# Two weight chunks in one matrix instruction for most tiles of queries, z and output; VectorE takes part in the last splits

## The chip, the cores and the metric

One core of a Trainium2 chip runs the whole kernel. The metric is device time in microseconds, the median of several executions. Every duration below is of one profiled execution.

## The reference, cut to what matters

One layer, 1024 tokens of width 1024, all float32. A normalised h (1024 x 1024) is multiplied by one wide weight matrix w_in whose columns are split into eleven parts; two branches follow and are merged:

```python
proj = h @ w_in[layer]
(u_a, z_a, q, k, v, z_b, q_idx, k_idx, w_idx, g_a, g_b) = jnp.split(proj, split_points, axis=-1)
y_a = multiscale_pool(u_a, ...) * silu(z_a)
q = rope(rmsnorm(q)); k = rope(rmsnorm(k)); q_idx, k_idx = rope(q_idx), rope(k_idx)
attn = dsa_sparse_attention(q, k, v, q_idx, k_idx, w_idx)   # scores with relu, top 256 keys, softmax
y_b = attn * silu(z_b)
merged = sigmoid(g_a) * (y_a @ w_branch_a) + sigmoid(g_b) * (y_b @ w_branch_b)
x = x + gate * (merged @ w_out)
```

q and z_b have 512 columns each, w_out is 1024 x 1024.

## The kernel before, in words

**Numbers in two parts.** Every float32 operand of a large product is split into a high part (rounded by a copy into the matrix format) and a low part (the rest). A product is three matrix instructions, high x high, high x low, low x high (lines 680 to 682, function `product`). For weights, ScalarE makes the high part (line 617, `split_piece_hi`) and GpSimd the low part (line 622, `split_piece_lo`); VectorE does it for the first four pieces alone (`split_piece_v`).

**Chunks, pieces, slots.** Weights come in chunks of 256 columns (`CW`), numbered in the order of use; a chunk of 1024 rows is two pieces of 128 x 4 x 256, loaded by SyncE into one of three raw buffers (`load_piece`), which is free again once the low part is made. The parts of a chunk stand in slot (ci - 1) % 2 of `w_hi` and `w_lo`. So chunk ci + 2 can be split only when the last product with chunk ci is done (`chunk_done`, waited for in `split_chunk_hi`). The two chunks of q, the two of z_b, and w_out's chunks 0 and 1, and 2 and 3, are neighbours and fill slots 0 and 1.

**Tiles of rows.** For q, z_b and the output, 128 tokens are the stationary operand and 256 weight columns the moving one: 8 steps of k, three instructions each, into half of a PSUM bank. The banks `pp[0]` and `pp[1]` alternate; a list `pp_uses` fixes the order of their uses, and `pp_claim` waits until the last user of the bank was evicted. The other products (`channels`) have weights as stationary and 512 tokens as moving operand.

**Order of the stages on TensorE.** (1) k, v and the index parts. (2) Scoring: six blocks b = 2 to 7 of eight heads each. A head is one product of index queries with (b + 1) x 128 keys into `ps`; ScalarE applies relu (line 1209), VectorE adds it into the score (lines 1850, 1853). After each head TensorE does two steps of a q tile (`q_step`, `Q_STEPS` = 2): 16 steps, two narrow tiles, a block. At head 5 it transposes the index queries of the next block (line 809), which GpSimd must have split (`qi_split_lo`, line 1458), in its queue behind the finishing of a q tile (`finish_query`), which follows VectorE's normalisation of that tile, whose last step is `query_gain` (line 1840) at head 7. (3) z_b: all eight tiles of chunk 0, then all eight of chunk 1; ScalarE applies silu (line 1176) and stores them to memory; after four tiles it takes square roots for the last four query tiles, which VectorE and GpSimd then finish before VectorE begins the bisection for the 256th score (line 1877). GpSimd's queue here is: low parts of z chunk 0, the causal select of the last scores (line 1489, waits for VectorE's last score), low parts of z chunk 1, the last query tiles, low parts of ua 0 and gb 0. (4) 20 chunks of h products (ua, gb, za, ga), the tie masks in between (`mask_products`; VectorE writes `eq`, line 1912, TensorE transposes it, line 885). (5) Attention. (6) Branch b: 16 units of 12 wide instructions; VectorE merges each (lines 1984 and 1986), ScalarE makes the high part of the merged unit (`mT_hi`, line 1393), GpSimd its low part (`mT_lo`, line 1627). m_raw has four buffers, freed by the low part. (7) Output: four chunks one after another, eight tiles each; TensorE first waits for 14 of the 16 merged units. VectorE multiplies by the gate (line 2028, this frees the bank), adds the row of x (line 2031), ScalarE issues the store. The splits of the next chunks are ScalarE's and GpSimd's.

Of the kernel before, what the change touches and what calls it, by code (L numbers as in the profile page):

```python
# [23 lines left out]
P = 128  # L24
# [15 lines left out]
CW = 256  # L40
# [26 lines left out]
def hybrid_layer(nc, x, c, positions, w_ada, b_ada, norm_gain, w_in, w_pool_group, pool_scale,  # L67
# [106 lines left out]
    for i in range(4):  # L174
        pp_uses += [("wo", i, t) for t in range(NT)]
# [17 lines left out]
    def chunk_done(ci):  # L193

        name = [k for k, v in name_of.items() if v == ci][0]
        kind, i = name if isinstance(name, tuple) else (name, 0)
        return max(pp_sig[n] for n, use in enumerate(pp_uses)
                   if use[:2] == (kind, i) or (kind == "za" and use[:2] == ("mix", i)))
# [48 lines left out]
    with ExitStack() as ctx:  # L247
# [78 lines left out]
        def tenants_a(s):  # L326
# [12 lines left out]
            with ExitStack() as k:  # L339
                zb_out = alloc(k, "zb_out", [P, 4, CW])  # L340
# [4 lines left out]
        def tenants_c(s):  # L345
# [10 lines left out]
            with ExitStack() as k:  # L356
                x_row, o_row = alloc(k, "x_row", [P, 4, CW]), alloc(k, "o_row", [P, 4, CW])
# [77 lines left out]
        m_raw_done, mT_hi_done, mT_lo_done = sem("m_raw_done"), sem("mT_hi_done"), sem("mT_lo_done")  # L435
# [30 lines left out]
        def _(sp):  # L466
# [70 lines left out]
            def load_x_row(n):  # L537
                i, t = n // NT, n % NT
                if n >= 4:
                    sp.wait_ge(o_row_done, n - 3)  # L540
                sp.dma_start(x_row[:, n % 4, :], x[t * P:(t + 1) * P, i * CW:(i + 1) * CW]).then_inc(x_row_in[n % 4], 16)
# [10 lines left out]
            for i in range(4):  # L552
                sp.wait_ge(zb_spilled[i], 16 * 4)
# [96 lines left out]
        Q_STEPS = 2  # L650
        assert Q_STEPS * NSEL * H == (2 * NT - Q_FIRST) * KD
# [7 lines left out]
        def _(pe):  # L659
# [24 lines left out]
            def rows_step(o, t, ci, k, width):  # L684

                s, tok = slot(ci), slice(t * P, (t + 1) * P)
                if ci == name_of["kv"]:
# [3 lines left out]
                               w_hi[:, s, k, 0:width], w_lo[:, s, k, 0:width], k == 0, k == KD - 1)  # L691

# [128 lines left out]
            def q_step(n):  # L821
                (i, t), k = Q_ORDER[n // KD], n % KD
                ci = name_of[("q", i)]
# [3 lines left out]
                last = rows_step(o, t, ci, k, CW)  # L827
# [201 lines left out]
            pe.wait_ge(mT_lo_done, 14)  # L1029
            for i in range(4):  # L1030
                ci = name_of[("wo", i)]
                pe.wait_ge(w_lo_done, pieces_through[ci])
                for t in range(NT):
                    if i == 0 and t == NT // 2:
                        pe.wait_ge(mT_hi_done, 16)
                        pe.wait_ge(mT_lo_done, 16)
                    o = pp_claim(("wo", i, t))
                    tok = slice(t * P, (t + 1) * P)
                    for k in range(KD):
                        last = product(o[:, 0:CW], mT_hi[:, k, tok], mT_lo[:, k, tok], w_hi[:, slot(ci), k, :],  # L1040
                                       w_lo[:, slot(ci), k, :], k == 0, k == KD - 1)
                    last.then_inc(pp_full, 1)
# [3 lines left out]
        def _(act):  # L1046
# [124 lines left out]
            def zb_tile(i, t):  # L1171
                s = (i * NT + t) % 4
                if i * NT + t >= 4:
                    act.wait_ge(zb_spilled[s], 16 * ((i * NT + t) // 4))
# [26 lines left out]
            for b in range(FREE_BLOCKS, NT):  # L1201
                for h in range(H):
# [14 lines left out]
                    step += Q_STEPS  # L1217
# [16 lines left out]
            for s in range(4):  # L1234
                act.wait_ge(zb_spilled[s], 16 * 4)
# [173 lines left out]
        def _(pool):  # L1409
# [98 lines left out]
            for s in range(4):  # L1508
                pool.wait_ge(zb_spilled[s], 16 * 4)
# [119 lines left out]
            for i in range(4):  # L1629
                split_chunk_lo(pool, name_of[("wo", i)] + 2)  # L1630
# [3 lines left out]
        def _(dve):  # L1634
# [182 lines left out]
            def query_squares(t):  # L1817
                dve.wait_ge(pp_free_a, pp_at[("q", 1, t)] + 1)
# [233 lines left out]
```

## Time and profile before

| | us |
|---|---|
| median of 3 runs | 843.44 (843.12 to 843.59) |
| the profiled execution | 841.9 |
| its span, first to last instruction | 839.7 |
| TensorE busy | 803.0 (96%) |
| VectorE busy | 569.2 (68%) |
| GpSimd busy | 380.6 (45%) |
| ScalarE busy | 351.2 (42%) |

The profiled time is the span and 2.2 us around it. In the rows, PE is TensorE's matmuls, PEld its weight loads, DVE VectorE, ACT ScalarE, POOL GpSimd, SP SyncE. Matmul records overlap, since the engine is pipelined: the distance from start to start is the pace. "[1.08 <-issue]" at a row's end is the idle time before it and what ended it.

### The profile page before, as it was taken

The numbers are of one execution on the slowest core, as the hardware profiler recorded it, in microseconds if no ns is written. First come the engines' busy times: TensorE is split into PE (matmuls) and PEld (weight loads), VectorE is DVE, ScalarE is ACT, GpSimd is POOL, SyncE is SP. The second block draws the span as 40 slices with busy tenths as digits, with TensorE's granted clock in tenths as the row PEclk, the third lists the DMA queues.
The fourth block names the chain that finished last, engine by engine and source line by source line (L and its number), as shares of the span: only waits on it lengthen the run. The fifth ranks groups of instructions, "written<-read, shape, count | busy, mean of one in ns | idle before, by whom it ended". The sixth has DMA issues, their size and how long they took to land.

```text
span 839.7 us, 13949 instructions
## 1 busy us (share of the span) xinstructions
PE 803.0 (96%) x4978; PEld 707.9 (84%) x4978; DVE 569.2 (68%) x1193; ACT 351.2 (42%) x647; POOL 380.6 (45%) x333
## 2 busy tenths in 40 slices
PE   3899999999999999999999999989999999999998
PEld 3699998889998888887878877778788887889998
DVE  5845538978888888898898636446557885654332
ACT  6473346665222222223242223676777883420000
POOL 1024544335624467861652212754887812982200
PEclk9899999999999999999999999999999999999999
DMA  9930110004332220331122323632433114744332
GB/s 350 378 90 14 51 51 14 27 13 126 124 102 64 90 79 32 98 99 42 51 88 88 100 98 117 218 122 89 141 110 95 46 37 140 247 138 135 120 93 73
DMA packets 62685, 87.95 MB, mean 105 GB/s; under 512 B 5881, under 2 KB 44317, under 8 KB 61726
## 3 DMA queue, kind: packets, MB, share of 16 engines
q1 hardware_dynamic: 48606, 64.04, 24.5%
q10 hardware_dynamic: 12096, 16.78, 5.6%
q0 software_dynamic: 1920, 6.29, 2.0%
q8 instruction: 40, 0.66, 0.3%
q14 instruction: 23, 0.19, 0.1%
HBM read 66.12 MB, written 20.97 MB: 104 GB/s over the span
## 4 chain that ended last, share of the span: by engine, by line
PE 86%; ACT 4%; DVE 3%; DMA 3%; issue 2%; SPq 1%; POOL 0%; DVEq 0%; ACTq 0%
PE pp L680 23%; PE pp L682 22%; PE pp L681 22%; PE pp L1007 3%; PE ps L818 3%; PE ps L817 3%; PE pt L973 3%; DMA ada_w<-in_w_ada 2%; ACT a_out L1311 1%; SPq L490 1%; DVE prob L1998 1%; DVE pT L1940 1%; PE ps L749 1%; PE pt L919 1%; ACT w_hi L617 1%
## 5 line engine op out<-in xcount | busy, mean ns | idle before, releaser
L622 POOL TENSOR_TENSOR w_lo<-w_raw,w_hi 128x1024 fp32r<-128x1024 f32 x50 | 123.6, 2490 | 216.8 <-ACT w_hi L617 165.1
L1877 DVE TENSOR_SCALAR_CACHE_REDUCE junk<-score,cand 128x384 uint8<-128x384 f32 (+1 forms) x186 | 168.6, 944 | 19.3 <-issue 13.3
L680 PE MATMUL pp<-hT_hi,w_hi 128*128 128x512 f32 x384 | 150.2, 391 | 0.0
L682 PE MATMUL pp<-hT_hi,w_lo 128*128 128x512 f32 x384 | 149.5, 389 | 0.0
L681 PE MATMUL pp<-hT_lo,w_hi 128*128 128x512 f32 x384 | 149.4, 389 | 0.0
L680 PE MATMUL pp<-w_hi,hT_hi 128*128 128x256 f32 x352 | 101.2, 287 | 0.5 <-ACT zb_out L1176 0.5
L682 PE MATMUL pp<-w_hi,hT_lo 128*128 128x256 f32 x352 | 99.4, 282 | 0.0
L681 PE MATMUL pp<-w_lo,hT_hi 128*128 128x256 f32 x352 | 99.4, 282 | 0.0
L1940 DVE TENSOR_TENSOR pT<-pt,pT 128x512 fp32r<-128x512 f32 (+3 forms) x96 | 50.5, 554 | 53.2 <-ACT pT L1361 50.4
L680 PEld LDWEIGHTS pp<-hT_hi,w_hi 128*128 128x128 f32 x384 | 72.1, 188 | 16.0 <-issue 0.8
L682 PEld LDWEIGHTS pp<-hT_hi,w_lo 128*128 128x128 f32 x384 | 72.1, 188 | 15.2
L681 PEld LDWEIGHTS pp<-hT_lo,w_hi 128*128 128x128 f32 x384 | 72.1, 188 | 14.7
L680 PE MATMUL pp<-w_hi,mT_hi 128*128 128x256 f32 x256 | 72.5, 283 | 0.6 <-ACT mT_hi L1393 0.6
L617 ACT ACTIVATE w_hi<-w_raw 128x1024 fp32r<-128x1024 f32 x52 | 52.6, 1052 | 47.6 <-DVE o_row L2031 43.4
L681 PE MATMUL pp<-w_lo,mT_hi 128*128 128x256 f32 x256 | 72.4, 283 | 0.0
L682 PE MATMUL pp<-w_hi,mT_lo 128*128 128x256 f32 x256 | 72.4, 283 | 0.0
L1247 ACT ACTIVATE stage<-pp 128x512 f32<-128x512 f32 x32 | 19.1, 598 | 126.7 <-PE pp L682 126.7
L680 PEld LDWEIGHTS pp<-w_hi,hT_hi 128*128 128x128 f32 x352 | 67.1, 191 | 1.6 <-ACT zb_out L1176 0.7
L681 PEld LDWEIGHTS pp<-w_lo,hT_hi 128*128 128x128 f32 x352 | 67.2, 191 | 0.7
L682 PEld LDWEIGHTS pp<-w_hi,hT_lo 128*128 128x128 f32 x352 | 67.1, 191 | 0.0
L680 PE MATMUL pp<-yT_hi,w_hi 128*128 128x512 f32 x128 | 52.5, 410 | 1.1 <-ACT a_out L1311 1.1
L1853 DVE SCALAR_TENSOR_TENSOR score<-rel,w_idx,score 128x384 f32<-128x384 f32 (+5 forms) x42 | 46.8, 1114 | 10.0 <-ACT rel L1209 6.6
(275 smaller groups left out, 1817.2 us busy)
## 6 DMA issues: line engine op xcount, KB each, us to landing
w_raw<-in_w_in SPq DMA_DIRECT2D x36, 512.0 KB, 3.8
ada_w<-in_w_ada SPq DMA_DIRECT2D x7, 1024.0 KB, 11.6
sgb_spill<-stage ACTq DMA_DIRECT2D x16, 256.0 KB, 2.0
sga_spill<-stage ACTq DMA_DIRECT2D x16, 256.0 KB, 2.0
stage<-sga_spill SPq DMA_DIRECT2D x16, 256.0 KB, 3.2
ma_spill<-stage POOLq DMA_DIRECT2D x16, 256.0 KB, 2.4
gate_w<-in_w_ada SPq DMA_DIRECT2D x16, 256.0 KB, 2.7
w_raw<-in_w_out SPq DMA_DIRECT2D x8, 512.0 KB, 4.5
```

The lines of the kernel that those rows point to most:

```text
L617: nc.scalar.activation(hi, raw, ACT.Copy).then_inc(w_hi_done, 1)
L622: nc.gpsimd.tensor_tensor(lo, raw, hi.bitcast(F32), ALU.subtract).then_inc(w_lo_done, 1)
L680: nc.tensor.matmul(o, a_hi, b_hi, start=first, stop=False)
L681: nc.tensor.matmul(o, a_hi, b_lo, start=False, stop=False)
L682: return nc.tensor.matmul(o, a_lo, b_hi, start=False, stop=last)
L817: nc.tensor.matmul(o[:, a:z], q, kt_[:, 0, a:z], start=True, stop=False)
L818: last = nc.tensor.matmul(o[:, a:z], q, kt_[:, 1, a:z], start=False, stop=True)
L973: last = nc.tensor.transpose(o[:, (t % 4) * P:(t % 4 + 1) * P], prob[j % 4][:, t * P:(t + 1) * P], ident[:])
L1007: last = nc.tensor.matmul(pp[0][:, 0:2 * P], v2[:, t, :], pT[:, u % 2, t, s, :, :].rearrange("p h q -> p (h q)"), start=(t == 0 and s == 0 ...
L1853: ins = v.scalar_tensor_tensor(s, rel[:, n % 2, 0:keys(b)], w, s, ALU.mult, ALU.add)
L1877: v.tensor_scalar(junk[:, n % 2, 0:keys(b)], score[:, score_at(b):score_at(b + 1)], least, None, ALU.is_ge, ALU.add, accum_out=cnt[:, n:n ...
L1940: v.tensor_tensor(pT[:, j // 2 % 2, t0:t1, 1, j % 2, :], pt[n % 2][:, 0:(t1 - t0) * P].rearrange("p (t q) -> p t q", q=P), pT[:, j // 2 % ...
```

## The change

For tiles 2 to 6 of q, 2 to 7 of z_b and 2 to 7 of the output (for w_out's chunks 0 and 1, then 2 and 3), one instruction takes both slots as moving operand: 512 columns, two pieces of 256 in `w_hi[:, :, k, :]`, into a whole bank (`pair_step`). The others stay narrow and stand around the pairs: of z_b (0,0), (0,1) ahead and (1,0), (1,1) behind; of the output the same for each pair of chunks. During scoring a head of blocks 2 to 6 has one wide step instead of two narrow ones; block 7 keeps two narrow ones. Evictions, row buffers (`zb_out`, `x_row`, `o_row`), loads and stores of pairs have 512 columns. ScalarE splits ua 0 after the last z pair. The low parts of merged units with odd number, and of w_out's chunks 1, 2 and 3, go from GpSimd to VectorE; VectorE makes those of chunk 2 just ahead of evicting the last pair of chunks 0 and 1, those of chunk 3 ahead of evicting tile (1, 1). GpSimd's queue around z_b is as it was.

```diff
-    Q_ORDER = [(0, 0), (0, 1), (1, 0), (1, 1)] + [(i, t) for t in range(2, NT) for i in range(2)]
+    BOTH = (0, 1)
+    Q_ORDER = [(0, 0), (0, 1), (1, 0), (1, 1)] + [(BOTH, t) for t in range(2, NT - 1)] + [(0, NT - 1), (1, NT - 1)]
     Q_FIRST = 4
     pp_uses += [("q", i, t) for i, t in Q_ORDER]
-    for i in range(2):
-        pp_uses += [("zb", i, t) for t in range(NT)]
+    ZB_ORDER = [(0, 0), (0, 1)] + [(BOTH, t) for t in range(2, NT)] + [(1, 0), (1, 1)]
+    pp_uses += [("zb", i, t) for i, t in ZB_ORDER]
+    ZB_SLOTS = [16 * len(ZB_ORDER[s::4]) for s in range(4)]
+    WO_ORDER = []
+    for i in (0, 2):
+        WO_ORDER += [(i, 0), (i, 1)] + [((i, i + 1), t) for t in range(2, NT)] + [(i + 1, 0), (i + 1, 1)]
+
+    def first_of(i):
+        return i[0] if isinstance(i, tuple) else i
+
+    def width_of(i):
+        return 2 * CW if isinstance(i, tuple) else CW
...
-        m_raw_done, mT_hi_done, mT_lo_done = sem("m_raw_done"), sem("mT_hi_done"), sem("mT_lo_done")
+        m_raw_done, mT_hi_done = sem("m_raw_done"), sem("mT_hi_done")
+        mT_lo_v, mT_lo_p = sem("mT_lo_v"), sem("mT_lo_p")
...
-            for n in range(4 * NT - 4):
-                if n == 4:
+            for n in range(len(WO_ORDER) - 4):
+                if n == 2:
                     load_piece(nxt)
                     load_piece(nxt + 1)
-                if n == NT + 4:
+                if n == 7:
                     for m in range(nxt + 2, len(pieces)):
                         load_piece(m)
                 load_x_row(n + 4)
...
-        Q_STEPS = 2
-        assert Q_STEPS * NSEL * H == (2 * NT - Q_FIRST) * KD
+        Q_STEPS = {b: 1 if b < NT - 1 else 2 for b in range(FREE_BLOCKS, NT)}
+        assert sum(Q_STEPS.values()) * H == (len(Q_ORDER) - Q_FIRST) * KD
...
+            def pair_step(o, act_hi, act_lo, t, k):
+
+                tok = slice(t * P, (t + 1) * P)
+                return product(o[:], act_hi[:, k, tok], act_lo[:, k, tok], w_hi[:, :, k, :], w_lo[:, :, k, :],
+                               k == 0, k == KD - 1)
...
-                last = rows_step(o, t, ci, k, CW)
+                last = pair_step(o, hT_hi, hT_lo, t, k) if i == BOTH else rows_step(o, t, ci, k, CW)
...
-                    for _ in range(Q_STEPS):
+                    for _ in range(Q_STEPS[b]):
...
-            for i in range(2):
-                for t in range(NT):
-                    rows_tile("zb", i, t, first=t == 0)
+            for i, t in ZB_ORDER:
+                if i != BOTH:
+                    rows_tile("zb", i, t, first=(i, t) == (0, 0))
+                    continue
+                pe.wait_ge(w_lo_done, pieces_through[name_of[("zb", 1)]])
+                o = pp_claim(("zb", i, t))
+                for k in range(KD):
+                    last = pair_step(o, hT_hi, hT_lo, t, k)
+                last.then_inc(pp_full, 1)
...
-            pe.wait_ge(mT_lo_done, 14)
-            for i in range(4):
-                ci = name_of[("wo", i)]
-                pe.wait_ge(w_lo_done, pieces_through[ci])
-                for t in range(NT):
-                    if i == 0 and t == NT // 2:
-                        pe.wait_ge(mT_hi_done, 16)
-                        pe.wait_ge(mT_lo_done, 16)
-                    o = pp_claim(("wo", i, t))
-                    tok = slice(t * P, (t + 1) * P)
-                    for k in range(KD):
+            pe.wait_ge(mT_lo_v, 7)
+            pe.wait_ge(mT_lo_p, 7)
+            for i, t in WO_ORDER:
+                pair = isinstance(i, tuple)
+                ci = name_of[("wo", i[-1] if pair else i)]
+                if t == (2 if pair else 0):
+                    pe.wait_ge(w_lo_done, pieces_through[ci])
+                if t == NT // 2:
+                    pe.wait_ge(mT_hi_done, 16)
+                    pe.wait_ge(mT_lo_v, 8)
+                    pe.wait_ge(mT_lo_p, 8)
+                o = pp_claim(("wo", i, t))
+                tok = slice(t * P, (t + 1) * P)
+                for k in range(KD):
+                    if pair:
+                        last = pair_step(o, mT_hi, mT_lo, t, k)
+                    else:
                         last = product(o[:, 0:CW], mT_hi[:, k, tok], mT_lo[:, k, tok], w_hi[:, slot(ci), k, :],
                                        w_lo[:, slot(ci), k, :], k == 0, k == KD - 1)
-                    last.then_inc(pp_full, 1)
+                last.then_inc(pp_full, 1)
...
-            for i in range(2):
-                for t in range(NT):
-                    zb_tile(i, t)
-                    if (i, t) == (0, 3):
-                        for late in NORM_LATE:
-                            query_root(late)
-                split_chunk_hi(act, name_of[("zb", i)] + 2)
+            for n in range(len(ZB_ORDER)):
+                zb_tile(n)
+                if n == 3:
+                    for late in NORM_LATE:
+                        query_root(late)
+                if n == len(ZB_ORDER) - 3:
+                    split_chunk_hi(act, name_of[("zb", 0)] + 2)
+            split_chunk_hi(act, name_of[("zb", 1)] + 2)
...
-            for n in range(4 * NT):
-                i, t = n // NT, n % NT
+            for n, (i, t) in enumerate(WO_ORDER):
+                if i == BOTH and t == NT - 1:
+                    split_chunk_hi(act, name_of[("wo", 2)])
+                if (i, t) == (1, 1):
+                    split_chunk_hi(act, name_of[("wo", 3)])
                 act.wait_ge(o_row_done, n + 1)
-                act.dma_start(out[t * P:(t + 1) * P, i * CW:(i + 1) * CW], o_row[:, n % 4, :]).then_inc(stored[n % 4], 16)
-                if t == NT - 1:
-                    split_chunk_hi(act, name_of[("wo", i)] + 2)
+                c0, w = first_of(i) * CW, width_of(i)
+                act.dma_start(out[t * P:(t + 1) * P, c0:c0 + w], o_row[:, n % 4, 0:w]).then_inc(stored[n % 4], 16)
...
-                if n in WB_LAST:
+                if n in WB_LAST and n < 15:
                     split_chunk_lo(pool, name_of[("wb", WB_LAST[n])] + 2)
-                pool.wait_ge(mT_hi_done, n + 1)
-                gp.tensor_tensor(mT_lo[:, 2 * i + m, tok], m_raw[:, n % 4, :], mT_hi[:, 2 * i + m, tok].bitcast(F32),
-                                 ALU.subtract).then_inc(mT_lo_done, 1)
-            for i in range(4):
-                split_chunk_lo(pool, name_of[("wo", i)] + 2)
...
-                    dve.wait_ge(mT_lo_done, n - 3)
+                    dve.wait_ge(*((mT_lo_v, (n - 3) // 2) if n % 2 else (mT_lo_p, (n - 2) // 2)))
...
+            def merge_low(n):
+                i, m, f = UNITS_B[n]
+                tok = slice(f * HALF, (f + 1) * HALF)
+                dve.wait_ge(mT_hi_done, n + 1)
+                v.tensor_tensor(mT_lo[:, 2 * i + m, tok], m_raw[:, n % 4, :], mT_hi[:, 2 * i + m, tok].bitcast(F32),
+                                ALU.subtract).then_inc(mT_lo_v, 1)
+
+            def split_chunk_v(ci):
+                for n, (cj, _) in enumerate(pieces):
+                    if cj == ci:
+                        dve.wait_ge(w_lo_done, n)
+                        split_piece_v(n)
...
+                if n % 2 == 0:
+                    merge_low(n - 1)
+            merge_low(15)
+            split_chunk_v(name_of[("wo", 1)])
+
+            for n, (i, t) in enumerate(WO_ORDER):
+                if i == BOTH and t == NT - 1:
+                    split_chunk_v(name_of[("wo", 2)])
+                if (i, t) == (1, 1):
+                    split_chunk_v(name_of[("wo", 3)])
+                u = pp_at[("wo", i, t)]
+                c0, w = first_of(i) * CW, width_of(i)
+                if (i, t) in ((0, 0), (2, 0)):
+                    dve.wait_ge(pt_free_a, pt_done[pt_at[("gate", i // 2)]][0])
...
-                v.tensor_tensor(o_row[:, n % 4, :], pp[pp_bank[u]][:, 0:CW], gate[:, i * CW:(i + 1) * CW],
+                v.tensor_tensor(o_row[:, n % 4, 0:w], pp[pp_bank[u]][:, 0:w], gate[:, c0:c0 + w],
                                 ALU.mult).then_inc(pp_free_v, 1)
                 dve.drain()
-                v.tensor_tensor(o_row[:, n % 4, :], o_row[:, n % 4, :], x_row[:, n % 4, :], ALU.add).then_inc(o_row_done, 1)
+                v.tensor_tensor(o_row[:, n % 4, 0:w], o_row[:, n % 4, 0:w], x_row[:, n % 4, 0:w], ALU.add).then_inc(o_row_done, 1)
```

## Rows read from the trace of the kernel before

**Rows 1.** Page, part 4: the chain that ended last, by engine.

```profile
PE 86%; ACT 4%; DVE 3%; DMA 3%; issue 2%; SPq 1%; POOL 0%; DVEq 0%; ACTq 0%
```

**Rows 2.** Windows: stretch, length, busy (instructions) of each engine, clock, DMA share, GB/s.

```profile
142.00:155.00 13.00, 12.38 (x93) 11.56 (x92) 11.88 (x20) 7.89 (x14) 5.31 (x7) 1.00 0.06 22
```

**Rows 3.** Timeline of TensorE before and in the output: start, length, line, operands.

```profile
737.84 0.39 PE L680 MATMUL pp<-yT_hi,w_hi 128*128 128x512 f32 x1
...
742.60 0.39 PE L680 MATMUL pp<-yT_hi,w_hi 128*128 128x512 f32 x1
...
744.46 0.28 PE L680 MATMUL pp<-w_hi,mT_hi 128*128 128x256 f32 x1
...
747.69 0.28 PE L680 MATMUL pp<-w_hi,mT_hi 128*128 128x256 f32 x1
```

**Rows 4.** Timeline, three engines, 168 to 176 us: end of scoring block 5.

```profile
168.69 0.68 DVE L1840 TENSOR_TENSOR q_all<-q_all,gains 128x512 f32<-128x512 f32 x1
...
173.87 1.27 POOL L1458 TENSOR_TENSOR qi_stk<-qi,qi_stk 128x512 fp32r<-128x512 f32 x1
...
175.24 0.84 PE L809 MATMUL pt<-ident_r,qi_stk 128*128 128x128 f32 x8 [1.08 <-issue]
```

**Rows 5.** Timeline, VectorE and GpSimd, 195 to 248 us.

```profile
195.05 2.67 DVE L1853 SCALAR_TENSOR_TENSOR score<-rel,w_idx,score 128x1024 f32<-128x1024 f32 x2
...
197.93 0.78 POOL L1489 TENSOR_SCALAR_AFFINE_SELECT score<-score 128x128 f32<-128x128 f32 x1 [4.07 <-DVEq L1858]
...
198.69 5.26 POOL L622 TENSOR_TENSOR w_lo<-w_raw,w_hi 128x1024 fp32r<-128x1024 f32 x2
...
242.62 4.77 POOL L622 TENSOR_TENSOR w_lo<-w_raw,w_hi 128x1024 fp32r<-128x1024 f32 x2 [13.73 <-ACT w_hi L617]
```

**Rows 6.** Timeline of TensorE at its third z tile.

```profile
199.98 0.38 PE L680 MATMUL pp<-w_hi,hT_hi 128*128 128x256 f32 x1 [0.45 <-ACT zb_out L1176]
```

**Rows 7.** Instructions on the tie masks eq: duration min/median/max, first and last start.

```profile
L885 PE MATMUL pt<-ident_b,eq x33: 219/219/230, 487.3 to 521.3; 128*128 128x128 bf16 x33
...
L1912 DVE TENSOR_SCALAR eq<-score,thr x6: 414/582/750, 474.6 to 519.8; 128x384 bf16<-128x384 f32 x1, 128x512 bf16<-128x512 f32 x1, 128x640 bf16<-128x640 f32 x1, 128x768 bf16<-128x768 f32 x1
```

**Rows 8.** Timeline, ScalarE and GpSimd, around the last tiles of z 0.

```profile
217.60 0.38 ACT L1176 ACTIVATE zb_out<-pp 128x256 f32<-128x256 f32 x1 [2.50 <-PE pp L682]
...
218.45 2.01 ACT L617 ACTIVATE w_hi<-w_raw 128x1024 fp32r<-128x1024 f32 x2 [0.46 <-ACT zb_out L1176]
...
241.49 2.01 ACT L617 ACTIVATE w_hi<-w_raw 128x1024 fp32r<-128x1024 f32 x2 [0.46 <-ACT zb_out L1176]
...
256.93 0.60 ACT L1259 ACTIVATE ua<-pp 128x512 f32<-128x512 f32 x1 [4.84 <-PE pp L682]
...
224.13 4.76 POOL L622 TENSOR_TENSOR w_lo<-w_raw,w_hi 128x1024 fp32r<-128x1024 f32 x2
```

**Rows 9.** Timeline, all four engines, last merge and first output tile.

```profile
739.25 5.94 POOL L1627 TENSOR_TENSOR mT_lo<-m_raw,mT_hi 128x512 fp32r<-128x512 f32 x4
...
743.48 2.01 ACT L617 ACTIVATE w_hi<-w_raw 128x1024 fp32r<-128x1024 f32 x2
...
743.48 0.69 DVE L1984 TENSOR_TENSOR m_raw<-pp,e_in 128x512 f32<-128x512 f32 x1 [0.69 <-PE pp L682]
...
744.03 0.36 PE L680 MATMUL pp<-w_hi,mT_hi 128*128 128x256 f32 x1 [0.59 <-ACT mT_hi L1393]
...
744.27 1.47 DVE L1986 TENSOR_TENSOR m_raw<-m_raw,e_in 128x512 f32<-128x512 f32 x1
...
745.77 0.63 ACT L1393 ACTIVATE mT_hi<-m_raw 128x512 fp32r<-128x512 f32 x1 [0.27 <-DVE m_raw L1986]
```

**Rows 10.** Instructions that write w_lo, VectorE's: duration min/median/max in ns.

```profile
L1708 DVE TENSOR_TENSOR w_lo<-w_raw,w_hi x2: 1218/1222/1225, 47.8 to 50.0; 128x1024 fp32r<-128x1024 f32 x2
```

**Rows 11.** Windows (columns of rows 2): the stretch of the lower clock.

```profile
40.00:46.00 6.00, 5.68 (x28) 5.71 (x29) 5.27 (x11) 5.76 (x11) 0.00 (x0) 0.54 0.26 75
```

**Rows 12.** Waits of TensorE: us in total, times, longest us.

```profile
PE ps L988 <- ACT oT L1338: 5.5, 6, 1.4
```

More of the change, by code:

```diff
@@ L173, in hybrid_layer @@
     pp_uses += [("wb", i, (m, f)) for i, m, f in UNITS_B]
-    for i in range(4):
-        pp_uses += [("wo", i, t) for t in range(NT)]
+    pp_uses += [("wo", i, t) for i, t in WO_ORDER]
     pp_bank += [(n + 1) % 2 for n in range(len(pp_uses) - len(pp_bank))]
@@ L197, in chunk_done @@
         return max(pp_sig[n] for n, use in enumerate(pp_uses)
-                   if use[:2] == (kind, i) or (kind == "za" and use[:2] == ("mix", i)))
+                   if use[:2] == (kind, i) or (kind == "za" and use[:2] == ("mix", i))
+                   or (use[0] == kind and isinstance(use[1], tuple) and i in use[1]))
     pt_uses = [("cols", "v"), ("gains", "v")]
@@ L339, in tenants_a @@
             with ExitStack() as k:
-                zb_out = alloc(k, "zb_out", [P, 4, CW])
+                zb_out = alloc(k, "zb_out", [P, 4, 2 * CW])
             alloc(s, "zone_k", [P, 8 * 256])
@@ L356, in tenants_c @@
             with ExitStack() as k:
-                x_row, o_row = alloc(k, "x_row", [P, 4, CW]), alloc(k, "o_row", [P, 4, CW])
+                x_row, o_row = alloc(k, "x_row", [P, 4, 2 * CW]), alloc(k, "o_row", [P, 4, 2 * CW])
             alloc(s, "zone_c", [P, 16 * 256])
@@ L552, in _ @@
             for i in range(4):
-                sp.wait_ge(zb_spilled[i], 16 * 4)
+                sp.wait_ge(zb_spilled[i], ZB_SLOTS[i])
             load_q(0)
@@ L822, in q_step @@
                 (i, t), k = Q_ORDER[n // KD], n % KD
-                ci = name_of[("q", i)]
+                ci = name_of[("q", first_of(i))]
                 if t == 0 and k % 4 == 0:
@@ L1169, in qi_copies, with zb_tile @@
                                          ACT.Copy).then_inc(pt_free_a, 1)
[L1171 to L1174, printed above, removed]
+            def zb_tile(n):
+                (i, t), s = ZB_ORDER[n], n % 4
+                c0, w = first_of(i) * CW, width_of(i)
+                if n >= 4:
+                    act.wait_ge(zb_spilled[s], 16 * (n // 4))
                 o = pp_take(("zb", i, t))
-                nc.scalar.activation(zb_out[:, s, :], o[:, 0:CW], ACT.Silu).then_inc(pp_free_a, 1)
+                nc.scalar.activation(zb_out[:, s, 0:w], o[:, 0:w], ACT.Silu).then_inc(pp_free_a, 1)
                 act.wait_ge(pp_free_a, pp_at[("zb", i, t)] + 1)
-                act.dma_start(zb_dram[t * P:(t + 1) * P, i * CW:(i + 1) * CW], zb_out[:, s, :]).then_inc(zb_spilled[s], 16)
+                act.dma_start(zb_dram[t * P:(t + 1) * P, c0:c0 + w], zb_out[:, s, 0:w]).then_inc(zb_spilled[s], 16)
             for i, t in LATE:
@@ L1216, in _ @@
                         qi_copies(b + 1)
-                    step += Q_STEPS
+                    step += Q_STEPS[b]
                     if step % KD == 0:
@@ L1234, in _ @@
             for s in range(4):
-                act.wait_ge(zb_spilled[s], 16 * 4)
+                act.wait_ge(zb_spilled[s], ZB_SLOTS[s])
             def stage_slot(n):
@@ L1508, in _ @@
             for s in range(4):
-                pool.wait_ge(zb_spilled[s], 16 * 4)
+                pool.wait_ge(zb_spilled[s], ZB_SLOTS[s])
             def window_mean(g):
@@ L1623, in _ @@
                 tok = slice(f * HALF, (f + 1) * HALF)
-                if n in WB_LAST:
+                if n in WB_LAST and n < 15:
                     split_chunk_lo(pool, name_of[("wb", WB_LAST[n])] + 2)
-                pool.wait_ge(mT_hi_done, n + 1)
-                gp.tensor_tensor(mT_lo[:, 2 * i + m, tok], m_raw[:, n % 4, :], mT_hi[:, 2 * i + m, tok].bitcast(F32),
-                                 ALU.subtract).then_inc(mT_lo_done, 1)
-            for i in range(4):
-                split_chunk_lo(pool, name_of[("wo", i)] + 2)
+                if n % 2 == 0:
+                    pool.wait_ge(mT_hi_done, n + 1)
+                    gp.tensor_tensor(mT_lo[:, 2 * i + m, tok], m_raw[:, n % 4, :], mT_hi[:, 2 * i + m, tok].bitcast(F32),
+                                     ALU.subtract).then_inc(mT_lo_p, 1)
         @block.vector
@@ L2017, in _ @@
                 merge(n)
-            for n in range(4 * NT):
-                i = n // NT
-                u = pp_at[("wo", i, n % NT)]
-                if n % (2 * NT) == 0:
-                    dve.wait_ge(pt_free_a, pt_done[pt_at[("gate", n // (2 * NT))]][0])
+                if n % 2 == 0:
+                    merge_low(n - 1)
[7 more added lines that the diff above has]
+                u = pp_at[("wo", i, t)]
+                c0, w = first_of(i) * CW, width_of(i)
+                if (i, t) in ((0, 0), (2, 0)):
+                    dve.wait_ge(pt_free_a, pt_done[pt_at[("gate", i // 2)]][0])
                 dve.wait_ge(pp_full, pp_sig[u])
```

11 lines of the change are left out of this document (6 added, 5 removed).

## The prediction

> **What bounds the kernel now.** Read the page first. TensorE is busy for 96% of the span (table above) and makes up 86% of the chain that ended last [rows 1]: time leaves only where TensorE issues less or waits less. Since its records overlap, the pace of a stretch is read from starts, not durations. One window says where TensorE does not set the pace alone: from 142 to 155 us, in the scoring stage, it is busy for 12.38 of 13 us and VectorE for 11.88, so VectorE's queue is nearly full there [rows 2].
>
> **The unit of the gain.** In the output stage 27 instructions of 256 columns start between 744.46 and 747.69, 119.7 ns apart; just before, 21 of 512 columns start between 737.84 and 742.60, 226.7 ns apart [rows 3]. Two narrow ones cost 239.3 to 240 ns, a wide one 226.7: 13.3 ns saved by each fusion. A tile of rows has 8 x 3 = 24 instructions: 2.88 us narrow, 5.44 us wide, so a fused pair saves 0.32 us. There are 5 pairs of queries, 6 of z and 12 of output: 23 x 0.32 = 7.4 us if all lay on the path. No row shows a moving operand in two pieces (two slots, apart in memory): from no extra cost to the whole saving lost (two narrow instructions, 240 ns). I take none, since weight loads and matmuls are otherwise the same.
>
> The Trainium skill (TensorE: Matmul & The Clock Gate, section Back-to-back issue gap) speaks against this change: it gives N/2.4 + 2.5 ns, thus 109 ns and 216 ns, only 2.5 ns per fusion and 1.4 us for all 23 pairs, with which this change would be about 5 us worse than my sum. The trace does not agree (119.7 and 226.7 ns for these operands), and it decides.
>
> **Queries.** Per scoring head two steps of 0.36 us become one of 0.68, 0.04 us less, in five blocks of eight heads; the last block keeps its narrow tiles. All 40 heads would be 1.6 us. But from 132 us to about 169 the order is set by VectorE: it ends the gain of block 5 at 169.37, GpSimd then finishes that query tile and splits the next index queries from 173.87, and TensorE, which had waited 1.08 us, starts its transposes at 175.24 [rows 4]. TensorE time saved within that chain is lost again. On the path lie the 8 heads of block 2, about 3 of block 3 and the last 3 of block 6: 14 x 0.04 = 0.5 us. Ends: 0.1 and 1.6. One copy of 512 columns (0.60 us) in place of two of 0.38 stays inside ScalarE's gaps.
>
> **z of branch b, the start.** Two narrow tiles are followed at once by pairs, which need both chunks. Before, the second chunk was needed only eight tiles later, and its low part was made accordingly: behind VectorE's last score (done 197.72) and the causal select at 197.93, GpSimd splits it from 198.69 to 203.95 [rows 5]. None of that is moved. TensorE started its third z tile at 199.98 [rows 6]; its first pair can start at about 204.03. New wait: 4.05 us. Behind it in TensorE's queue stands everything else.
>
> **z, the middle.** Six pairs save 6 x 0.32 = 1.92 us. ScalarE's square roots, four tiles in, come after two narrow tiles and two pairs in place of four narrow tiles: 4.05 + 2 x 2.56 = 9.2 us later. GpSimd then ends its last query at about 233 instead of 224 (where its next split began, [rows 8]), still ahead of its next split. VectorE's bisection starts 9 us later also, while TensorE's mask products move by some 3 us: the first ties were ready at 474.6 + 0.4 and read at 487.3 [rows 7], so 12 us of cover shrink to about 6. Nothing is paid, but that cover is halved.
>
> **z, the end.** The next chunk (ua 0) takes the slot of z 0, which now is free only after the last pair, at T; two narrow tiles (5.76 us) cover its split instead of eight. ScalarE starts an eviction 0.34 us after the last issue (217.60 against 199.98 + 6 x 2.88), and its split 0.85 us after that [rows 8]; with a 512-column eviction (0.60 in place of 0.38) the first high piece starts at T + 1.4. GpSimd began 1.13 us after it (242.62 against 241.49) and took 4.77 us for both pieces [rows 5, 8]: low part ready at T + 7.3, TensorE restarts at T + 7.36. Wait: 1.6 us. Sum of z: 4.05 - 1.92 + 1.6 = +3.7 us.
>
> **Merge and the start of the output.** GpSimd's four low splits between 739.25 and 745.19 held TensorE back to 744.03; the last issue slot ended at 743.29 (742.60 + 3 x 0.23) [rows 3, 9]. Now GpSimd has half of them and VectorE the others, one of 0.69 us per two units while its own unit takes about 1.6 of 2.72 us. With GpSimd's chunk splits running, its additions stretch (0.69 to 1.47 us) [rows 9], and it may lag by a unit; two banks allow that. I take the old wait of 0.74 us as gone (ends: gone, or doubled). What is late next is wo 1, needed after two tiles: ScalarE's high part ends at 745.49, the last mT high at 746.15, VectorE's last low part at 746.85, then two splits of 1.22 us each [rows 9, 10] end at 749.3, and only then is tile 0 evicted (0.42): its bank is free at 749.8, when the first pair wants to start at 743.29 + 5.76 = 749.05. Wait: 0.8 us.
>
> **The seams in the output.** Twice VectorE is told to split a chunk ahead of an eviction. After the last pair of chunks 0 and 1, at T: first high piece ready at T + 1.35, two low pieces until T + 3.8, eviction of the pair 0.69 (a 512-column one with a PSUM source, [rows 9]) until T + 4.5. TensorE fills the other bank with one narrow tile (2.88 us) and then waits 1.67 us for that bank. After tile (1, 1) the same with wo 3 and an eviction of 0.42: 4.27 - 2.88 = 1.39 us. Before, these splits were GpSimd's and no wait stood there. Twelve pairs save 3.84 us. Sum of the output: -0.74 + 0.8 - 3.84 + 1.67 + 1.39 = -0.7 us. The tail after the last matmul is that of a narrow tile, as before. The wider x and output rows have their loads four tiles ahead, over 10 us for a load of a few us: nothing.
>
> **Sum.** -0.5 + 3.7 - 0.7 = +2.5 us. The profiled execution took 841.9 us (span 839.7 and 2.2 around it): 844.4. The median of the runs is 1.54 above that execution: 845.9 us.
>
> **Rivals.** (a) The clock falls in the new 4 us wait. From 40 to 46 us, while the first products ran, the granted clock averaged 0.54, nearly all of it at the 1.2 GHz level; it cost (1 - 0.54) x 6 = 2.8 us [rows 11]. For it or against it the dense part shows nothing: its longest wait is 1.4 us [rows 12]. Time: 848.7, or about 851 if the fall lasts twice as long. The Trainium skill (the same page, section Why this matters for your kernels) warns that idle gaps between bursts of matmuls bring the lower clock back; no row here shows it in the dense part.
> (b) More of the query gain counts: VectorE is only 91% busy from 142 to 155 [rows 2], and its slow operations are collisions with GpSimd, which may shift. All 1.6 us: 844.8. Against: TensorE's 1.08 us before the transposes [rows 4], which a faster TensorE only lengthens.
> (c) The other side: the later waits are not paid. Each of the three seams (end of z, the two of the output) is a race of a split against narrow tiles set there as cover. If ScalarE and VectorE start earlier than these rows let them, or the second bank hides the split, 1.6 + 1.67 + 1.39 = 4.66 us fall away: 841.2, faster. It decides from 4.2 us on, so all three must go. Against: each start is taken from a row of the same code.
> (d) The two-piece operand costs as much as two narrow instructions: the 6.3 us of savings counted above are gone, 852.
>
> **How the numbers follow.** About 0.2% (1.7 us) is what a measurement of this kernel can tell from no change. Forecast 0.52, own range 844.9 to 847; (a) 0.15; (b) 0.19; (c) 0.09; (d) 0.05. Faster (below 841.75) is (c): 0.09. Same is (b) and 0.05 of the forecast, which lies only 0.8 us above the line: 0.24. Slower is the rest of it, (a) and (d): 0.67. The range, 843.2 to 849.6, takes in (b) and the short form of (a), and leaves (c) and (d) out.
>
> **What the new profile must show.** TensorE waits about 4 us for GpSimd's split of the second z chunk near 199.5 us, and about 1.6 us for ua 0 near 242. In the output, waits of about 1.7 and 1.4 us for VectorE's evictions behind its splits, and under 1 us before the first pair. Wide instructions over two slots at 226.7 ns. The stages from ua 0 to branch b keep their lengths (to 0.3 us). Granted clock 1.00 from 46 us on. I am wrong if the first z wait is under 3 us, if the clock falls, or if the wide pace is not 227 ns.

## The result, and the profile after

The changed kernel takes 848.02 us (median of 6 runs), the kernel before 843.25 beside it: ratio 1.0055, 95% interval 1.0038 to 1.0072. By the ratio it is slower by 4.6 us (the medians differ by 4.8), where 2.5 were forecast. Its profiled execution took 847.93 us with a span of 845.1.

The page first (busy time by engine; the chain by engine). TensorE runs 552 instructions fewer (4426 for 4978) and its share of the chain falls from 86% [rows 1] to 82%, while GpSimd now has 2%: something waits for it. The order in a row is that of the page: busy us, share of the span, number of instructions.

```profile
PE 800.4 (95%) x4426; PEld 681.5 (81%) x4426; DVE 565.7 (67%) x1183; ACT 349.7 (41%) x636; POOL 352.3 (42%) x319
...
PE 82%; ACT 5%; DVE 4%; DMA 3%; issue 2%; POOL 2%; SPq 1%; DVEq 1%; ACTq 0%; POOLq 0%
```

TensorE's waits name the places (us in total, times, longest; answers to [rows 12], where neither GpSimd's w_lo nor VectorE's o_row was listed):

```profile
PE pp L693 <- POOL w_lo L635: 5.7, 2, 4.4
...
PE ps L1013 <- ACT oT L1372: 5.6, 6, 1.4
...
PE pp L693 <- DVE o_row L2083: 2.8, 3, 1.5
```

**Stage by stage.** The span is cut at the starts of TensorE's instructions; lengths in us:

| stretch on TensorE | before | after | difference | forecast |
|---|---|---|---|---|
| start to the first scoring product | 117.74 | 119.37 | +1.63 | 0 |
| first to last scoring product | 74.64 | 74.25 | -0.39 | -0.5 |
| last scoring product to ua 0 (z) | 48.00 | 53.07 | +5.07 | +3.7 |
| ua 0 to the last merge product | 502.68 | 502.56 | -0.12 | 0 |
| last merge product to first of output | 0.97 | 0.42 | -0.55 | -0.74 |
| first to last start in the output | 92.10 | 91.86 | -0.24 | 0 |

The whole loss is in z. The first line is no work of the change; it is taken up at the end. Without it the lines add up to 3.77 us in this execution.

z, timelines of GpSimd and TensorE (answers to [rows 5, 6]): the select, the low part of z chunk 1, that of ua 0, and TensorE's start of ua 0.

```profile
199.15 0.78 POOL L1525 TENSOR_SCALAR_AFFINE_SELECT score<-score 128x128 f32<-128x128 f32 x1 [4.07 <-DVEq L1893]
...
199.90 5.17 POOL L635 TENSOR_TENSOR w_lo<-w_raw,w_hi 128x1024 fp32r<-128x1024 f32 x2
...
241.91 4.73 POOL L635 TENSOR_TENSOR w_lo<-w_raw,w_hi 128x1024 fp32r<-128x1024 f32 x2 [5.81 <-ACT w_hi L630]
...
246.69 0.50 PE L693 MATMUL pp<-hT_hi,w_hi 128*128 128x512 f32 x1 [1.34 <-POOL w_lo L635]
```

The low part of z chunk 1 ends at 205.07; TensorE, idle for 4.39 us, starts its first pair at 205.13. The chain behind that split goes further back than GpSimd. ScalarE's high part stands behind a relu, which had waited for VectorE's scores:

```profile
196.25 1.03 ACT L1242 ACTIVATE rel<-ps 128x1024 f32<-128x1024 f32 x1 [2.32 <-DVE score L1888]
...
197.44 2.01 ACT L630 ACTIVATE w_hi<-w_raw 128x1024 fp32r<-128x1024 f32 x2
```

Then comes what the forecast left to a rival. TensorE, five starts of that pair:

```profile
205.13 0.79 PE L693 MATMUL pp<-w_hi,hT_hi 128*128 128x512 f32 x1 [4.39 <-POOL w_lo L635]
...
205.72 0.63 PE L694 MATMUL pp<-w_lo,hT_hi 128*128 128x512 f32 x1
...
208.28 0.46 PE L694 MATMUL pp<-w_lo,hT_hi 128*128 128x512 f32 x1
...
208.57 0.39 PE L695 MATMUL pp<-w_hi,hT_lo 128*128 128x512 f32 x1
...
208.80 0.40 PE L693 MATMUL pp<-w_hi,hT_hi 128*128 128x512 f32 x1
```

From 205.72 to 208.28 six instructions start 427 ns apart, later ones 227 to 235. The windows say why (columns of [rows 2]; the second line is the stretch of [rows 2] in the changed kernel):

```profile
204.00:209.00 5.00, 3.87 (x10) 3.10 (x11) 4.00 (x7) 0.00 (x0) 1.07 (x1) 0.66 0.64 194
...
142.00:155.00 13.00, 12.21 (x67) 10.40 (x66) 11.88 (x19) 7.86 (x15) 5.31 (x7) 1.00 0.05 21
```

In 204 to 209 the granted clock averages 0.66: between its two levels of 1.2 and 2.4 GHz (0.50 and 1.00) that is 3.4 of the 5 us at the lower one. VectorE's 11.88 busy us in the scoring window are the same as before, TensorE's fell from 12.38 to 12.21: there most of the saving did not shorten the stage (-0.39 us of a possible 1.6), as forecast.

The seams in the output, VectorE's and TensorE's timelines:

```profile
789.91 2.49 DVE L1743 TENSOR_TENSOR w_lo<-w_raw,w_hi 128x1024 fp32r<-128x1024 f32 x2 [5.12 <-ACT w_hi L630]
...
792.31 0.68 DVE L2083 TENSOR_TENSOR o_row<-pp,gate 128x512 f32<-128x512 f32 x1
...
793.05 0.39 PE L693 MATMUL pp<-w_hi,mT_hi 128*128 128x256 f32 x1 [1.47 <-DVE o_row L2083]
...
797.38 2.49 DVE L1743 TENSOR_TENSOR w_lo<-w_raw,w_hi 128x1024 fp32r<-128x1024 f32 x2 [2.75 <-ACT w_hi L630]
...
799.78 0.42 DVE L2083 TENSOR_TENSOR o_row<-pp,gate 128x256 f32<-128x256 f32 x1
...
800.25 0.39 PE L693 MATMUL pp<-w_hi,mT_hi 128*128 128x256 f32 x1 [1.20 <-DVE o_row L2083]
```

Each time the two splits (2.49 us together) stand ahead of the eviction that TensorE's next tile needs. The pace of wide instructions over two slots, and the first pair's start:

```profile
755.82 0.47 PE L693 MATMUL pp<-w_hi,mT_hi 128*128 128x512 f32 x1 [0.16 <-DVE o_row L2083]
...
770.87 0.39 PE L693 MATMUL pp<-w_hi,mT_hi 128*128 128x512 f32 x1
...
779.03 0.39 PE L693 MATMUL pp<-w_hi,mT_hi 128*128 128x512 f32 x1
```

36 instructions in 8.16 us: 226.7 ns, the pace of [rows 3]; the operand in two pieces costs nothing. The masks (answers to [rows 7]):

```profile
L910 PE MATMUL pt<-ident_b,eq x33: 219/219/230, 493.7 to 527.7; 128*128 128x128 bf16 x33
...
L1947 DVE TENSOR_SCALAR eq<-score,thr x6: 417/582/750, 480.9 to 526.2; 128x384 bf16<-128x384 f32 x1, 128x512 bf16<-128x512 f32 x1, 128x640 bf16<-128x640 f32 x1, 128x768 bf16<-128x768 f32 x1
```

The first tie mask is ready at 481.3 (480.9 and 0.4) and read at 493.7, 12 us later; the cover did not shrink to 6.

### The profile page after: what moved, and what is told of

Its sections match the earlier page's. It is cut to its first block, busy times and chain, and to the rows that moved or that the text cites. A ratio compares the mean times of both kernels' runs of the same rounds, so it can differ in the third digit from the quotient of the medians.

```text
span 845.1 us, 12766 instructions
## 1 busy us (share of the span) xinstructions
PE 800.4 (95%) x4426; PEld 681.5 (81%) x4426; DVE 565.7 (67%) x1183; ACT 349.7 (41%) x636; POOL 352.3 (42%) x319
## 4 chain that ended last, share of the span: by engine, by line
PE 82%; ACT 5%; DVE 4%; DMA 3%; issue 2%; POOL 2%; SPq 1%; DVEq 1%; ACTq 0%; POOLq 0%
PE pp L693 22%; PE pp L695 21%; PE pp L694 21%; PE pp L1032 3%; PE pt L998 3%; PE ps L837 3%; PE ps L836 3%; DMA ada_w<-in_w_ada 2%; POOL w_lo L635 2%; ACT w_hi L630 1%; DVE score L1888 1%; ACT a_out L1345 1%; PE ps L768 1%; SPq L502 1%; DVE prob L2045 1%
## 5 line engine op out<-in xcount | busy, mean ns | idle before, releaser
L635 POOL TENSOR_TENSOR w_lo<-w_raw,w_hi 128x1024 fp32r<-128x1024 f32 x44 | 108.3, 2479 | 176.9 <-ACT w_hi L630 123.8
L693 PE MATMUL pp<-w_hi,hT_hi 128*128 128x256 f32 (+1 forms) x264 | 86.7, 329 | 4.4 <-POOL w_lo L635 4.4
L694 PE MATMUL pp<-w_lo,hT_hi 128*128 128x256 f32 (+1 forms) x264 | 84.7, 321 | 0.0
L695 PE MATMUL pp<-w_hi,hT_lo 128*128 128x256 f32 (+1 forms) x264 | 84.5, 320 | 0.0
L693 PE MATMUL pp<-w_hi,mT_hi 128*128 128x512 f32 (+1 forms) x160 | 55.8, 349 | 2.9 <-DVE o_row L2083 2.8
L693 PEld LDWEIGHTS pp<-w_hi,hT_hi 128*128 128x128 f32 x264 | 50.5, 191 | 7.6 <-POOL w_lo L635 4.6
L694 PE MATMUL pp<-w_lo,mT_hi 128*128 128x512 f32 (+1 forms) x160 | 55.5, 347 | 0.0
L695 PE MATMUL pp<-w_hi,mT_lo 128*128 128x512 f32 (+1 forms) x160 | 55.4, 346 | 0.0
L695 PEld LDWEIGHTS pp<-w_hi,hT_lo 128*128 128x128 f32 x264 | 50.5, 191 | 3.8
L694 PEld LDWEIGHTS pp<-w_lo,hT_hi 128*128 128x128 f32 x264 | 50.7, 192 | 2.6
```

The costliest lines, as they stand in the source:

```text
L635: nc.gpsimd.tensor_tensor(lo, raw, hi.bitcast(F32), ALU.subtract).then_inc(w_lo_done, 1)
L693: nc.tensor.matmul(o, a_hi, b_hi, start=first, stop=False)
L694: nc.tensor.matmul(o, a_hi, b_lo, start=False, stop=False)
L695: return nc.tensor.matmul(o, a_lo, b_hi, start=False, stop=last)
```

## The experiments

Each was timed beside the kernel before on the same chip. Ratios are to the kernel before, with their 95% intervals. The lengths of z (last scoring product to ua 0) and of the output (first to last start) are read as above.

| kernel | ratio | z, us | output, us | lower clock after the z wait |
|---|---|---|---|---|
| before | 1 | 48.00 | 92.10 | none |
| changed | 1.0055 (1.0038 to 1.0072) | 53.07 | 91.86 | 3.4 us |
| changed, again | 1.0045 (1.0031 to 1.0060) | 54.39 | 91.88 | 6.8 us |
| z: four narrow | 0.9963 (0.9951 to 0.9976) | 46.74 | 91.88 | none |
| z wait filled | 1.0024 (1.0011 to 1.0037) | 51.57 | 91.88 | none |
| eviction first | 1.0008 (0.9996 to 1.0020) | 54.35 | 88.71 | 6.8 us |
| output alone | 0.9987 (0.9975 to 0.9999) | 48.00 | 91.88 | none |
| GpSimd's order | 1.0032 (1.0020 to 1.0043) | 51.84 | 91.88 | 3.4 us |
| both mended | 0.9924 (0.9910 to 0.9939) | 46.74 | 88.70 | none |
| three narrow, all | 0.9926 (0.9913 to 0.9938) | 46.44 | 88.74 | none |

**Four narrow tiles of z on either side.**

```diff
-    ZB_ORDER = [(0, 0), (0, 1)] + [(BOTH, t) for t in range(2, NT)] + [(1, 0), (1, 1)]
+    ZB_ORDER = [(0, t) for t in range(4)] + [(BOTH, t) for t in range(4, NT)] + [(1, t) for t in range(4)]
...
-                    rows_tile("zb", i, t, first=(i, t) == (0, 0))
+                    rows_tile("zb", i, t, first=t == 0)
...
-                if n == len(ZB_ORDER) - 3:
+                if n == NT - 1:
```

> The changed kernel with four narrow tiles of z ahead of the pairs and four behind them, in place of two and two (four pairs in place of six). My theory: the first pair starts after GpSimd's split is done, so the wait of 4.4 us, the lower clock in it (1.5 us) and the 1.3 us wait at the end of z go, and two fusions (0.64 us) are given up: 6.1 us less than the changed kernel's 848, thus 842, under the kernel before (843.2). Rival (wide instructions over two slots are themselves slow somewhere): the waits go but the time stays at 846 or more. The granted clock must be 1.00 from 200 us on.

838.73 us against 841.63, 2.9 less where 1.2 less was expected: the longer form of the fall, seen further down, was not counted. z is 6.33 us shorter than in the changed kernel and 1.26 shorter than before: four fusions of 0.32, with nothing else left. TensorE's waits in z:

```profile
PE pp L693 <- ACT zb_out L1209: 0.5, 1, 0.5
```

That is the old wait of 0.45 us [rows 6] alone. So the waits for w_lo and the clock are the whole loss, and wide instructions over two slots are not slow; the rival falls.

**The z wait filled with unused products.**

```diff
+                if t == 2:
+                    n = ps_at[("idx", NT - 1, H - 2)]
+                    pe.wait_ge(ps_free_a, ps_done[n][0])
+                    for _ in range(18):
+                        nc.tensor.matmul(ps[n % 2][:, 0:512], ident_b[:], prefix[:, 0:512], start=True, stop=True)
                 pe.wait_ge(w_lo_done, pieces_through[name_of[("zb", 1)]])
```

> The changed kernel with 18 unused 512-column bf16 instructions (3.8 us) in the place of the 4.4 us wait before the first z pair; nothing else moves. My theory: idleness is what lowered the clock after the wait; with the wait filled the first pair runs at 226.7 ns from its start and 1.5 us are saved: 846.5, while the start of the first pair stays at 205 us. Rival (the clock falls there for another reason, or the seven slow instructions come from the start of a wide stretch): the slow instructions stay, 848.

```profile
200.82 3.83 PE L879 MATMUL ps<-prefix,ident_b 128*128 128x512 bf16 x17
...
205.16 0.50 PE L693 MATMUL pp<-w_hi,hT_hi 128*128 128x512 f32 x1 [0.50 <-POOL w_lo L635]
...
205.49 0.40 PE L694 MATMUL pp<-w_lo,hT_hi 128*128 128x512 f32 x1
...
205.73 0.39 PE L695 MATMUL pp<-w_hi,hT_lo 128*128 128x512 f32 x1
```

The first pair starts at the same time (205.16 for 205.13), but at 233 ns a step: the clock stays up, and z is 51.57 us, 1.50 less. The wait itself is unchanged in length, only busy. So idleness in it, not the wide stretch, brought the lower clock. The ratio went from 1.0055 and 1.0045 to 1.0024: 1.8 to 2.6 us, more than the 1.5 expected (its interval and that of 1.0045 overlap a little). That fits a fall that lasts twice as long in other executions, of which the next run shows one.

**The changed kernel again.**

> The changed kernel once more, beside the three others on the same chip. My theory: ratio 1.0055 again, with TensorE's clock at the lower level for 3.4 or 6.8 us after the first z wait in its profile. Rival (the fall was a matter of that one execution): ratio 1.002 to 1.003, no fall.

The fall is there again, and longer (columns of [rows 2]):

```profile
204.00:209.00 5.00, 3.86 (x9) 3.09 (x10) 4.01 (x7) 0.00 (x0) 1.08 (x1) 0.54 0.69 197
...
209.00:214.00 5.00, 5.00 (x19) 3.96 (x19) 0.00 (x0) 0.26 (x1) 0.00 (x0) 0.78 0.01 3
```

From 204.4 to 211.2 us the clock is at the lower level; z is 54.39 us, 2.8 more than with the filled wait. That the fall was a matter of one execution is refuted: all three profiles with this z order and queue order and the wait left idle show it (this one, the first, and the next kernel's). The timed executions agree: the mean granted clock over the span is 0.987 to 0.991 in all twelve of the changed kernel, 0.991 to 0.996 in the twelve with the filled wait.

**Eviction ahead of the splits.**

```diff
             for n, (i, t) in enumerate(WO_ORDER):
-                if i == BOTH and t == NT - 1:
-                    split_chunk_v(name_of[("wo", 2)])
-                if (i, t) == (1, 1):
-                    split_chunk_v(name_of[("wo", 3)])
...
                 v.tensor_tensor(o_row[:, n % 4, 0:w], o_row[:, n % 4, 0:w], x_row[:, n % 4, 0:w], ALU.add).then_inc(o_row_done, 1)
+                if i == BOTH and t == NT - 1:
+                    split_chunk_v(name_of[("wo", 2)])
+                if (i, t) == (1, 1):
+                    split_chunk_v(name_of[("wo", 3)])
```

> The changed kernel with VectorE's splits of output chunks 2 and 3 moved behind the eviction of the tile that they now stand ahead of. My theory: both waits of TensorE for the bank (1.47 and 1.20 us) go and no other takes their place, since the split ends at T + 4.0 us and is needed at T + 5.8: 845.3. Rival (the weights then come late, or the next eviction does): 847 to 848, with a wait of 1 us or more for w_lo or for the following tile's bank.

TensorE's waits in the whole output, and VectorE at the first seam:

```profile
PE pp L693 <- DVE o_row L2079: 0.2, 1, 0.2
...
789.87 0.69 DVE L2079 TENSOR_TENSOR o_row<-pp,gate 128x512 f32<-128x512 f32 x1 [3.96 <-PE pp L695]
...
791.26 2.48 DVE L1743 TENSOR_TENSOR w_lo<-w_raw,w_hi 128x1024 fp32r<-128x1024 f32 x2
...
793.66 0.42 DVE L2079 TENSOR_TENSOR o_row<-pp,gate 128x256 f32<-128x256 f32 x1
```

Evict, add, split, evict: the output falls from 91.86 to 88.71, by 3.15 us, with one wait of 0.2 us left. The two waits read as 1.47 and 1.20 us idle cost 3.15 together: the idle time counts from the end of the last record, which lasts 0.28 us, and not from the end of its slot of 0.12, and the first instruction after each wait takes 0.22 until the next start in place of 0.12. The forecast, made in slots (1.67 + 1.39), is nearer. By the ratios the gain is 4.0 us against the first timing of the changed kernel (1.0055 to 1.0008) and 3.1 against the second (1.0045).

**Only the output's part.**

```diff
-    Q_ORDER = [(0, 0), (0, 1), (1, 0), (1, 1)] + [(BOTH, t) for t in range(2, NT - 1)] + [(0, NT - 1), (1, NT - 1)]
+    Q_ORDER = [(0, 0), (0, 1), (1, 0), (1, 1)] + [(i, t) for t in range(2, NT) for i in range(2)]
...
-    ZB_ORDER = [(0, 0), (0, 1)] + [(BOTH, t) for t in range(2, NT)] + [(1, 0), (1, 1)]
+    ZB_ORDER = [(i, t) for i in range(2) for t in range(NT)]
...
-        Q_STEPS = {b: 1 if b < NT - 1 else 2 for b in range(FREE_BLOCKS, NT)}
+        Q_STEPS = {b: 2 for b in range(FREE_BLOCKS, NT)}
...
```

> Only the output's part of the change (pairs in the output, VectorE's share of the splits); queries and z as in the kernel before. My theory: the output stage gains 0.8 us net (3.84 of fusions and the old wait of 0.6, less 2.8 of new waits), nothing else changes and the clock does not fall at 200 us: 842.4. Rival (the loss is in the output or in the merge): 844 or more.

0.9987, -1.1 us (-0.1 to -2.1), and z is exactly 48.00 again. The output's part is a small gain, as forecast. No run has the queries' part or z's alone; what those do is read from the lengths of their stages.

**GpSimd's order.**

```diff
-            causal_scores(NT - 1)
             split_chunk_lo(pool, name_of[("zb", 1)])
+            causal_scores(NT - 1)
```

> The changed kernel with one exchange in GpSimd's queue: the low part of z chunk 1 ahead of the causal select of the last scores. My theory: the order of the queue is only part of the wait. ScalarE's high part of that chunk is ready at 198.5 us, so GpSimd starts at 198.6 in place of 199.9 and ends 1.3 us sooner; the wait shrinks from 4.4 to about 3.1 us and is not gone. If so short a wait also spares the lower clock (I think mostly), 3.5 us less than the changed kernel, ratio to the kernel before 1.001; if not, 1.3 us less. Rival (the queue order is the whole cause): the wait falls under 1 us, ratio 0.999 or less.

```profile
197.01 5.36 POOL L635 TENSOR_TENSOR w_lo<-w_raw,w_hi 128x1024 fp32r<-128x1024 f32 x2 [3.50 <-ACT w_hi L630]
...
202.32 0.82 POOL L1525 TENSOR_SCALAR_AFFINE_SELECT score<-score 128x128 f32<-128x128 f32 x1
...
202.42 0.80 PE L693 MATMUL pp<-w_hi,hT_hi 128*128 128x512 f32 x1 [3.25 <-POOL w_lo L635]
```

This execution is 1.6 us earlier at that point than the changed one. The split starts right after ScalarE's first high piece, yet TensorE still waits 3.25 us: the queue's order is 1.1 us of the wait. The rest is ScalarE's and GpSimd's own time and the late start of ScalarE's high part. And I was wrong that so short a wait would spare the clock:

```profile
202.00:206.00 4.00, 3.58 (x9) 2.86 (x10) 3.70 (x8) 0.00 (x0) 1.14 (x2) 0.57 0.83 252
```

The average of 0.57 over 202 to 206 us is 3.4 us at the lower level. So the ratio is 1.0032, not 1.001: 1.1 to 1.9 us less than the two timings of the changed kernel.

**Both mended.** The edits of "four narrow tiles" and of "eviction ahead of the splits" together.

> Both mended: four narrow tiles of z on either side (as in the run of that) and VectorE's eviction ahead of its splits. My theory: the two gains are in different stages and add: z 46.7 us from the last scoring product to ua 0, output 88.7 us from first to last start; against the kernel before -2.9 and -3.1, thus 6 us less: ratio 0.993. Rival (what is saved in z is given back in the output, as waits of the merge or of loads): under 4 us less.

```profile
PE pp L693 <- ACT zb_out L1209: 0.5, 1, 0.5
...
PE pp L693 <- DVE o_row L2079: 0.2, 1, 0.2
```

835.62 us against 841.82, -6.4 us. The two gains add. It beats the kernel before and the changed one.

**Three narrow tiles, with all.** Three in place of four, GpSimd's order exchanged, eviction first.

> All mended and one more pair kept: three narrow tiles of z on either side, GpSimd's exchanged order, eviction ahead of the splits. My theory: the third narrow tile ends at about the time at which the low part is ready (204 us), so no wait over 0.5 us, and one more fusion (0.32 us) than with four: 6.3 us less than the kernel before, ratio 0.9925. Rival: the first pair waits about 1 us and it is no better than with four.

```profile
PE pp L693 <- ACT zb_out L1209: 0.5, 1, 0.5
```

z is 46.44 us, 0.30 less than with four, and TensorE has no wait for w_lo in it; the ratios, 0.9926 and 0.9924, can't be told apart.

## Why the prediction was right, and where it was off

- **The time lies in the range, but not by the forecast's own sum, and to that extent it is luck.** What happened is rival (a), which had 0.15 of the chances. Its time of 848.7 is nearer to the measured 848.02 than the forecast's own 845.9, and a falling clock was one of the signs named for being wrong. The direction and the waits were worked out; that the measured time lies in the range is owed to the range having been drawn to take in the short form of (a).
- **The direction and the waits in z: right.** The first z pair waits for GpSimd's split, whose place in the queue nobody had moved. Without the clock, z is 3.57 us longer than before (51.57, filled); the sum gave 3.7. Its terms hold too: the first pair starts 3.91 us later after the last scoring product than the third z tile did (4.05 forecast), and between the last narrow tile's last slot and ua 0 lie 1.5 us (1.6 forecast).
- **The clock: the step that was off.** The sum took the wait to cost its own length only, and the fall stood beside it as rival (a) with 0.15. It fell in every profile of this order (3.4 us at the lower level, 1.5 us lost; or 6.8 and 2.8), and still after a wait of 3.25 us. This is the missing part: 2.5 forecast and 1.5 to 2.8 for the clock give 4.0 to 5.3, measured 4.6. By the rule on idle gaps (the Trainium skill, TensorE: Matmul & The Clock Gate, section Why this matters for your kernels) the fall was to be expected. The trace agrees: the clock fell to its lower level after idle waits of 3.25 and 4.39 us. I weighed it by what the dense part of the trace showed, where there was no wait long enough to test it; that absence was no evidence against.
- **The price of the fall** was set at 2.8 us from the start-up stretch; 1.5 and 2.8 were measured. Right in size.
- **The pace of fused instructions: right**, 226.7 ns. The Trainium skill's 216 ns for it (TensorE: Matmul & The Clock Gate, section Back-to-back issue gap), given there as the gap of an isolated instruction, is not what this kernel shows.
- **Queries: right in size.** 0.39 us of a possible 1.6 (0.5 forecast), so rival (b) falls. The idle times marked in TensorE's rows of that stage grew from 3.04 to 3.53 us, most of it ahead of the transposes as argued; the other 0.7 us lies in starts that are a little further apart, and its cause is not shown.
- **The seams: right.** 3.15 us for both by removing them, 3.06 forecast. The sum's own terms (4.5 - 2.88 and 4.2 - 2.88) give 1.62 and 1.34, not the 1.67 and 1.39 it wrote, a slip of 0.1 us in all. Rival (c) falls: none of the races was won.
- **The first output pair: too high.** 0.8 us forecast, 0.39 seen (755.82 against 749.67 + 5.76). And the wait before the output went from 0.74 to 0.19, not to nothing.
- **The cover of the masks: wrong and without effect.** The bisection started 12.1 us later than before (232.45 against 220.34; the scores themselves ended 1.2 later in this execution), but the first mask was ready only 6.3 us later, and so were its readers. What it regained lies in its small operations, the first threshold above all (before, then after):

```profile
225.70 3.24 DVE L1882 TENSOR_SCALAR thr<-cnt 128x6 int32<-128x6 f32 x1
...
237.81 0.17 DVE L1917 TENSOR_SCALAR thr<-cnt 128x6 int32<-128x6 f32 x1
```

Before, that operation ended as GpSimd's split did (224.13 and 4.76 [rows 8]); in the changed kernel no split of GpSimd's runs there. Over the whole bisection the 95 operations on 128x6 took 45.2 us in all for 51.0 before, which is the 5.8 us regained; all others together took the same (196.4 and 196.5). That the long ones are all collisions with GpSimd is not shown.

## What to carry to other kernels

A fused instruction that uses two chunks moves the need for the second chunk forward, and the need for their slots' next tenants back: look up, for each, in whose queue the work stands and what it stands behind, before counting what fusion saves. Narrow tiles at both ends are the cover, and their number is the knob. Where an engine both evicts and prepares, let it evict first. An idle wait of TensorE can cost more than its length: here those of 3.25 and 4.4 us did, those of up to 1.5 us did not.

## What the runs showed of the hardware

The lower clock comes after a wait of 3.25 us as well as of 4.4, in all four profiles with such a wait, and never after one of 1.5 us or less: from 50 us on the granted clock is 1.00 everywhere else in the ten profiles, up to the last products. No run has a wait between 1.5 and 3.25 us. The clock did not fall where unused bf16 products filled all but 0.5 us.

The lower clock also makes the start differ from execution to execution, whatever the kernel. The same products run there with the clock down for 6.8, 10.2 or 13.7 us, read from windows between 30 and 50 us. The two ends, in the window of 36 to 48 us, first of the kernel with four narrow z tiles, then of the changed one:

```profile
36.00:48.00 12.00, 10.84 (x70) 9.41 (x70) 9.80 (x19) 9.65 (x17) 0.00 (x0) 0.72 0.47 161
```

```profile
36.00:48.00 12.00, 10.83 (x47) 9.40 (x48) 8.26 (x17) 8.13 (x15) 0.00 (x0) 0.50 0.47 160
```

The first scoring product starts at 116.27 us in the one and 119.37 in the other, with the same instructions ahead of it (117.74 in the profile of before, [rows 11]). That is a spread of 3 us in single executions, larger than some parts of the change: spans of two profiles must not be compared before this stretch is taken out.
